# Longer strides between the slots of the split weights and the rows of the transposed gate product

## The reference, cut to what matters

```
swiglu(h, w_ffn_in, w_ffn_out):   a, b = split(h @ w_ffn_in, 2);  (silu(a) * b) @ w_ffn_out
first_block:   h @ w_mod;  project(h) = h @ w_in;  attention, retention;  mix @ w_out;  swiglu   (FFN 0)
second_block:  swiglu_2 (FFN 1);  h @ w_in, gated recurrence and convolution;  @ w_out
               memory attention: h @ w_q, mem @ w_kv, att @ w_o;  swiglu_2 (FFN 2);  rms_norm
FFN_HIDDEN = 2816, D_MODEL = 1024, SEQ = 256
```

## Time and profile before

| | |
|---|---|
| runs | 1239.74, 1243.00, 1243.35 us, median 1243.0 us |
| span of the profiled execution | 1239.3 us |
| TensorE busy | 1081.0 us (87%) |
| GpSimd, ScalarE, VectorE busy | 683.7, 493.5, 478.5 us |
| transfers | 188.70 MB, 152 GB/s over the span |

### The profile page before, as it was taken

The page is one execution under the profiler, slowest core; times in us unless marked ns, Lnnn a source line. Parts: engine busy times, 40 slices in busy tenths (PEclk is TensorE's granted clock), DMA queues, the critical chain, the costliest instruction groups (busy, mean ns, idle before and its releaser), DMA issues.

```text
span 1239.3 us, 13339 instructions
## 1 busy us (share of the span) xinstructions
PE 1081.0 (87%) x5056; PEld 883.5 (71%) x5056; DVE 478.5 (39%) x683; ACT 493.5 (40%) x582; POOL 683.7 (55%) x152
## 2 busy tenths in 40 slices
PE   6487897687874999999899999977978979999997
PEld 5376685466763888888688888767866767888885
DVE  5998858565866011100311110545643222111102
ACT  5424121524314444343544443553333624544431
POOL 4432324201312787878588878556434615988783
PEclk9686898889776999999899999998989989999999
DMA  6753543221421455545455555532312422555550
GB/s 247 262 214 126 204 179 127 98 72 68 160 78 66 144 197 171 201 170 197 138 191 187 185 176 198 198 135 103 135 69 72 156 79 102 204 189 184 184 190 34
DMA packets 26541, 188.70 MB, mean 152 GB/s; under 512 B 2944, under 2 KB 3200, under 8 KB 3968
## 3 DMA queue, kind: packets, MB, share of 16 engines
q1 hardware_dynamic: 25920, 185.63, 41.9%
q10 hardware_dynamic: 576, 2.43, 0.6%
HBM read 187.00 MB, written 1.05 MB: 152 GB/s over the span
## 4 chain that ended last, share of the span: by engine, by line
issue 37%; POOL 25%; PE 23%; DVE 9%; ACT 2%; DMA 2%; POOLq 0%; SPq 0%; DVEq 0%; ACTq 0%
POOL w_lo L559 25%; PE bank L1640 6%; PE bank L1642 6%; PE bank L1641 6%; DVE arena L1165 3%; DMA raw<-in_weights 1%; PE bank L1802 1%; DVE rows L1165 1%; PE bank L1813 1%; ACT w_hi L578 1%; PE bank L1851 1%; DVE shifted_T L1075 1%; DMA arena<-in_mem 1%; PE bank L1703 1%; DVE arena L1163 1%
## 5 line engine op out<-in xcount | busy, mean ns | idle before, releaser
L559 POOL TENSOR_TENSOR w_lo<-raw,w_hi 128x2048 fp32r<-128x2048 f32 x148 | 683.5, 4623 | 536.2 <-ACT w_hi L578 536.1
L578 ACT ACTIVATE w_hi<-raw 128x2048 fp32r<-128x2048 f32 x148 | 282.5, 1914 | 442.9 <-PE bank L1642 359.6
L1640 PE MATMUL bank<-w_hi,hT_hi 128*128 128x512 f32 (+1 forms) x928 | 378.3, 408 | 54.7 <-POOL w_lo L559 35.4
L1641 PE MATMUL bank<-w_lo,hT_hi 128*128 128x512 f32 (+1 forms) x928 | 369.1, 398 | 0.0
L1642 PE MATMUL bank<-w_hi,hT_lo 128*128 128x512 f32 (+1 forms) x928 | 368.8, 397 | 0.0
L1640 PEld LDWEIGHTS bank<-w_hi,hT_hi 128*128 128x128 f32 x928 | 181.4, 196 | 97.0 <-POOL w_lo L559 27.5
L1642 PEld LDWEIGHTS bank<-w_hi,hT_lo 128*128 128x128 f32 x928 | 180.0, 194 | 38.8
L1641 PEld LDWEIGHTS bank<-w_lo,hT_hi 128*128 128x128 f32 x928 | 181.5, 196 | 36.1 <-issue 0.2
L1640 PE MATMUL bank<-w_hi,gT_hi 128*128 128x512 f32 x264 | 104.9, 397 | 0.0
L1641 PE MATMUL bank<-w_lo,gT_hi 128*128 128x512 f32 x264 | 104.4, 395 | 0.0
L1642 PE MATMUL bank<-w_hi,gT_lo 128*128 128x512 f32 x264 | 104.4, 395 | 0.0
(11 more groups left out here) (244 smaller groups left out, 1039.7 us busy)
## 6 DMA issues: line engine op xcount, KB each, us to landing
raw<-in_weights SPq DMA_DIRECT2D x172, 1024.0 KB, 4.7
arena<-in_const ACTq DMA_DIRECT2D x1, 1088.0 KB, 5.0
arena<-in_mem SPq DMA_DIRECT2D x1, 1024.0 KB, 7.5
x_res<-in_x SPq DMA_DIRECT2D x1, 1024.0 KB, 7.0
arena<-in_ctx SPq DMA_DIRECT2D x1, 1024.0 KB, 6.8
out<-xn SPq DMA_DIRECT2D x2, 512.0 KB, 2.7
arena<-in_const SPq DMA_DIRECT2D x1, 770.0 KB, 6.2
rows<-in_final_norm ACTq DMA_DIRECT2D x1, 512.0 KB, 3.5
```

The costliest lines, as they stand in the source:

```text
L559: pool.tensor_tensor(w_lo[:, v_slot, :], raw[:, u_slot, :], w_hi[:, v_slot, :].bitcast(F32), ALU.subtract).then_inc(split_ready, 1)
L578: act.activation(w_hi[:, v_slot, :], raw[:, u_slot, :], ACT.Copy).then_inc(hi_ready, 1)
L1640: pe.matmul(out, hi, rhi, start=start, stop=False)
L1641: pe.matmul(out, hi, rlo, start=False, stop=False)
```

## The change

A slot of `w_hi` and `w_lo` becomes 2,052 elements long instead of 2,048, of which the last 4 are not used; a row of `gT_hi` and `gT_lo` 260 instead of 256. Small unused tensors are put behind `w_hi`, behind `w_lo` and ahead of `arena`. The reservation at the bottom is cut from 16,384 to 4,096 bytes, which makes room for it; no engine of the kernel starts a transfer that uses it. All instructions, their shapes, their order and their waits stay as they are; `gate` and `y_ffn` start 704 bytes further on in `arena`.

Where the operands start in a partition, as the programs place them, in bytes modulo 128:

| operand | before | after |
|---|---|---|
| `raw`, all slots | 0 | 0 |
| `w_hi`, `w_lo`, slot s | 0 | 16 s |
| `hT_hi`, `hT_lo`, each row | 0 | 0 |
| `hcT_hi`, `hcT_lo`, each row | 32 | 0 |
| `gT_hi`, row r | 32 | 16 r |
| `gT_lo`, row r | 32 | 96 + 16 r |
| `rows`, `xn`, `x_res` | 0 | 0 |
| start of `arena` | 32 | 0 |

Modulo 1,024 the first slots of `w_hi` and `w_lo` and the rows of `hT_hi` and `hT_lo` all start at 128 before (the whole tensors; rows are 1,024 bytes long); after, they start at 128, 256, 384 and 384.

```diff
+SKEW = 4
@@ the tensors
-        w_hi = sb("w_hi", [P, RING, UNIT], F32R)
-        w_lo = sb("w_lo", [P, RING, UNIT], F32R)
+        w_hi = sb("w_hi", [P, RING, UNIT + SKEW], F32R)
+        sb("gap_hi", [P, 16])
+        w_lo = sb("w_lo", [P, RING, UNIT + SKEW], F32R)
+        sb("gap_lo", [P, 16])
@@
         ARENA = 18440
+        sb("gap_arena", [P, 24])
@@
-        gT_hi = spot.enter_context(nc.sbuf_tensor("gT_hi", [P, 2 * UP, T], F32R))
-        gT_lo = spot.enter_context(nc.sbuf_tensor("gT_lo", [P, 2 * UP, T], F32R))
+        gT_hi = spot.enter_context(nc.sbuf_tensor("gT_hi", [P, 2 * UP, T + SKEW], F32R))
+        gT_lo = spot.enter_context(nc.sbuf_tensor("gT_lo", [P, 2 * UP, T + SKEW], F32R))
@@
-        gate = carve(2 * 2 * UP * T, 3, TB, 256)
-        y_ffn = carve(2 * 2 * UP * T + 3 * TB * 256, TB, D)
+        gate = carve(2 * 2 * UP * (T + SKEW), 3, TB, 256)
+        y_ffn = carve(2 * 2 * UP * (T + SKEW) + 3 * TB * 256, TB, D)
@@ GpSimd, L559
-                pool.tensor_tensor(w_lo[:, v_slot, :], raw[:, u_slot, :], w_hi[:, v_slot, :].bitcast(F32),
+                pool.tensor_tensor(w_lo[:, v_slot, 0:UNIT], raw[:, u_slot, :], w_hi[:, v_slot, 0:UNIT].bitcast(F32),
@@ ScalarE, L578
-                act.activation(w_hi[:, v_slot, :], raw[:, u_slot, :], ACT.Copy).then_inc(hi_ready, 1)
+                act.activation(w_hi[:, v_slot, 0:UNIT], raw[:, u_slot, :], ACT.Copy).then_inc(hi_ready, 1)
@@ gate_hi and gate_lo (L865, L1468): the same, rows cut to 0:T
@@
-    nc = _bacc.Bacc("TRN2", target_bir_lowering=False, num_devices=1)
+    nc = _bacc.Bacc("TRN2", target_bir_lowering=False, num_devices=1, dynamic_dma_scratch_size=4096)
```

More of the change, by code:

```diff
@@ L864, in gate_hi @@
                     act.wait_ge(bank_full[6], full)
-                    act.activation(gT_hi[:, at, :] if isinstance(at, slice) else gT_hi[:, bass.ds(at, 2), :],
+                    act.activation(gT_hi[:, at, 0:T] if isinstance(at, slice) else gT_hi[:, bass.ds(at, 2), 0:T],
                                    bank[6][:, :].rearrange("p (a t) -> p a t", t=T), ACT.Copy).then_inc(sem("gateT_hi"), 1)
@@ L1467, in gate_lo @@
                     s = at if isinstance(at, slice) else bass.ds(at, 2)
-                    dve.tensor_tensor(gT_lo[:, s, :], bank[6][:, :].rearrange("p (a t) -> p a t", t=T),
-                                      gT_hi[:, s, :].bitcast(F32), ALU.subtract).then_inc(bank_read[6], 1)
+                    dve.tensor_tensor(gT_lo[:, s, 0:T], bank[6][:, :].rearrange("p (a t) -> p a t", t=T),
+                                      gT_hi[:, s, 0:T].bitcast(F32), ALU.subtract).then_inc(bank_read[6], 1)
                 gated(0, silu0)
```

## The result

| | before | after |
|---|---|---|
| median | 1240.19 us (6 runs, 1235.61 to 1243.35) | 1246.11 us (6 runs, 1244.92 to 1248.95) |
| ratio | | 1.0053, 95% interval 1.0033 to 1.0073 |
| span of the profiled execution | 1239.3 us | 1244.0 us |

The changed kernel is slower by 0.53% (0.33% to 0.73%). The lines of the changed kernel are 4 further on: L1640 to L1642 are now L1644 to L1646, L559 is L563.

The account below looks back on a forecast made before the run. TensorE's matmul count times the step between starts was taken to bound the FFNs. Terms of -2.6, +5.3 and +2.0 summed to +4.7 us, added to the median 1243.0 for 1247.7; range 1222 to 1260, 8 in 10.

Parts of the forecast that it names:

- (1): gT in the FFN down halves: 792 matmuls go from 233.3 to 230.0 ns, -2.6 us.
- (2): hT in the up halves: slot 0 keeps 226.7 ns, 1,056 matmuls on slots 1 and 2 lose 5 ns, +5.3 us.
- (3): hT outside the FFNs: 800 matmuls on slots 1 and 2, half on the path, 5 ns each, +2.0 us.
- What bounds the kernel: In the FFNs, time is the number of TensorE matmuls times the step between starts; the others wait for TensorE.
- Two values of one matmul by its stationary operand's start: Upper clock: 226.7 ns on hT, starting at 0 modulo 128; 233.3 on hcT and gT, starting at 32.
- My reading of it: In SBUF, next weight load and current stream obstruct each other by their starts, losing 13.4 ns on hT, 20.0 on gT.
- rival B: Weight load and stream stop meeting on TensorE: all loss gone is 45 us, 1198; half, 1220; chance 0.18 with all halves.
- (4): ScalarE and GpSimd writing and reading slots that start at 16 or 32: taken at nothing.
- (5): The smaller reservation and the unused tensors: no instruction, so nothing.
- A: Whole kernel: the offsets change nothing, 1239.3 to 1246.7, say 1242 us; chance 0.22.
- C: Matmuls on slots 1 and 2: 10 ns more each, about 2,000 on the path, +20 us, 1263; chance 0.1.
- D: First 400 us: shifted GpSimd and VectorE instructions block each other differently, 5 us either way; no separate chance given.

Follow-up runs that it names:

- the probe without any other engine: Computes nothing of the reference: TensorE alone, groups of 24 float32r matmuls, only the operands' byte offsets changed; 227.8 ns at distance 0, 233.1 at 32.
- The bases alone: Kernel before with smaller reservation, w_lo 128 and hT 256 bytes further on, slot and row strides unchanged; ratio 1.0087 (1.0065 to 1.0109).
- the skew alone: Kernel before with smaller reservation, w_hi and w_lo slots 16 bytes longer, slot 0 and hT at one place modulo 1,024; ratio 1.0029 (1.0013 to 1.0046).
- the bases moved by 256: Kernel before with smaller reservation, w_lo 256 and hT 512 bytes further on, strides unchanged; ratio 1.0001 (0.9986 to 1.0015).
- the probe: TensorE alone, groups of 48 matmuls in the kernel's order with its operand offsets before and after; slot 0 after gave 231.0 ns once and 233.2 once.

## Why the prediction was right, and where its steps failed

The time and the sign held: 1247.7 us were forecast and 1246.11 measured, by a base that had come down by 2.8 us; +4.7 us were forecast, and +5.9 measured between the medians (0.53%, 0.33% to 0.73%), +4.7 between the profiled runs. That forecast and profiled runs agree at +4.7 is luck: terms (1) and (2) came to +2.7 where the rates give +5.7, and term (3) had +2.0 where the profiled runs have -0.8. The bounds of 1242 to 1256 also don't follow from the -9.3 and +15.6 stated ahead of them, which would be 1234 to 1259.

*What bounds the kernel*: right. The FFNs hold +5.5 us, and TensorE has no break in the up half of FFN 0 and 0.06 us of one in the down half. It waits 29.7 us in all for GpSimd's low part, 35.4 before.

*Two values of one matmul by its stationary operand's start*: right, and shown by moving only arena (0.9958, 233.3 to 227.0 ns) and by the probe without any other engine. *My reading of it*, that the load's reads are in the stream's way by where both start, doesn't hold as it stands: a load of one column loses no less than one of 128, and no distance is free of the loss. What stands behind it is open.

*(1) gT, -2.6 us*: the mechanism was right and the size off. A mixed set averages 231.5, not 230.0: -1.4 us, and a down unit took 5.56 us where 5.52 was named. I had taken the six steps behind one group of transposes for the average.

*(2) hT in the FFNs, +5.3 us*: this step failed in its condition. It let slot 0 keep 226.7 ns, since the table of starts modulo 128 showed 0 and 0, and gave slots 1 and 2 +5. Slot 0 went to 232.4, slots 1 and 2 to 231.0 and 232.2, all three +4.5 on average, 7.1 us. So the sign that was named, another value by slot and 226.7 in slot 0, failed; the chunk periods of a round do differ and average 11.57 us for the 11.5 named, but because the two values go by chunk. The period is 256 bytes and not 128, and the change puts w_hi and w_lo 128 bytes apart modulo 256, so one stream of each slot is at the wrong distance. The line on starts modulo 1,024 stood in the text on the change, and I used it for rival B alone. The bases alone cost 0.87%, the skew alone 0.29%; together with the skewed rows they don't add up but cost 0.53%. The rates say the same: hT loses no more with both (231.9 ns) than with the bases alone (232.2), and gT gains.

*(3) hT outside the FFNs, +2.0 us*: not shown. The profiled runs have -0.8 us outside the FFNs, and there the run with the reservation alone moves by 3 us from stage to stage with every distance as before. *(4) and (5)*, the writers and the reservation at nothing: right. VectorE has 749 and 752 ns, GpSimd 4,618 for 4,610, and the reservation alone gave 0.9992.

The rivals. A, nothing changes: out, hT and gT both moved. B, the two streams stop meeting: out, and not only for this layout; of all distances tried none is below 226.6 ns. C, the skew costs more than any distance of the trace: in the FFNs of these kernels no unit's matmuls average above 233.5 ns, so 242 was not reached. A start off the 16 bytes (both by 4, 237.7) would have come nearest. D: stages did move by some us, the one behind FFN 1, up to the first split of its output product, from 122.9 us to 119.6, and the next ones give it back. That stage has the same two lengths in runs whose hT and gT rates are those of before (119.7 with the reservation alone, 122.8 with the bases moved by 256), so the change need not be its reason. That blocked instructions cost it, as D has it, is not shown: the short runs have four GpSimd splits of over 4.7 us there and the long ones three.

On the rule of the Trainium skill, "SBUF — State Buffer", Who interferes with whom, that TensorE's two ports are independent and TensorE waits on nobody: for bfloat16 the runs agree (215.8 or 215.9 ns at each of three distances); for float32r they don't (226.6 to 234.3 by distance, alone on the core). "TensorE: Matmul & The Clock Gate" of the Trainium skill, Back-to-back issue gap, gives columns / 2.4 + 2.5 ns for a matmul by itself, an estimate of 215.8 for 512. In these runs bfloat16 measures just that with a weight load each, and float32r 226.7 at best. For a stream of weight load and matmul pairs the section gives about 131 ns at 512 columns. No run here comes near it, and the measurement decides.

## What to carry to other kernels

A layout with room between the slots isn't free of cost for a TensorE that is the bound: measure the step from matmul to matmul for each pair of operands before and after, since one of them got better here and hid part of the other's loss. For float32r operands and streams of 512 columns, start the stationary and every moving tile at one place modulo 256 bytes, on a multiple of 32, and keep strides at multiples of 256; "on 128 bytes" was worth nothing here. The best kernel of this study is before with 992 unused bytes ahead of arena and the smaller reservation: 0.9958 of before, and some 0.9% under the change.

## What the runs showed of the hardware

- A float32r matmul of 512 columns with its weight load takes 226.7 ns at best at 2.4 GHz, not 213.3, and up to 234.3 by the distance of the two starts modulo 256 bytes. On hT at 1.2 GHz nothing is lost (426.7 ns).
- The loss is per matmul: a load of 1 column has it (231.5 ns), a stream of 320 columns too (146.4 ns for 133.3). At 384 and 256 columns distance 32 is no worse than 0 (173.5 and 118.4 ns for 174.5 and 120.1). bfloat16 has 215.8 or 215.9 at all three distances tried.
- The same offsets can run in two rhythms, 231.0 or 233.2 ns in the probe, behind different groups. In the kernel after, the chunk periods of 11.64, 11.53 and 11.53 us are these two; with the bases alone FFN 2 has the slow one in every chunk and FFN 0 and 1 in every third. What picks the rhythm is open.
